# Decoder block on one core: projections, recurrence and attention in one stream over two token halves instead of three stages

## What is computed

```python
h = rmsnorm(x, norm_gain)
proj = h @ w_in                                    # 2048 x 6528
r, k, v, wd, ad, g = split(token_shift_lerp(p, mu))      # RWKV columns
decay = exp(-exp(w_log));  a = sigmoid(a0 + ad @ a_up);  kk = normalised k * k_k
# per head, per token:
sa = -S @ kk_t
S = S * w_t + outer(sa, b_t) + outer(v_t, k_t)
y = S @ r_t
y = groupnorm(y) * gain + bias + bonus;  y_rwkv = y * silu(g)
# attention: window 128, two kv heads, ALiBi slopes, a sink in the softmax
o = softmax([q k^T / 8 - slope * dist, sink]) @ v;  y_attn = o * silu(g)
out = rmsnorm(x + concat(y_rwkv, y_attn) @ w_out, final_gain)
```

## Time and profile before

| | |
|---|---|
| runs shown, median (lowest to highest) | 2253.88 us (2248.12 to 2255.84) |
| profiled execution: span, first to last instruction | 2249.4 us |
| outside the span, by the median | 4.5 us |
| PE, DVE, ACT, POOL busy in the span | 91%, 43%, 28%, 15% |
| DMA | 234 MB, mean 104 GB/s |

### The profile page before, as it was taken

One profiled execution on the slowest core, in us unless ns is written; L12 is line 12 of the kernel. 1 busy time (PEld: TensorE's weight loads), 2 busy tenths in 40 slices (PEclk: granted clock), 3 DMA queues, 4 the chain that ended last, 5 costly groups with the idle time before them and its releaser, 6 DMA issues. The chain is left out here.

```text
span 2249.4 us, 32629 instructions
## 1 busy us (share of the span) xinstructions
PE 2049.3 (91%) x12099; PEld 1715.2 (76%) x12099; DVE 965.8 (43%) x1225; ACT 620.1 (28%) x1295; POOL 327.2 (15%) x453
## 2 busy tenths in 40 slices
PE   6999999999999999999995788898889849998995
PEld 5788888888888888888884688787788737786874
DVE  5434243432434334343442565566566543334223
ACT  5321212112121121211210254344444443332331
POOL 1200000000000000000002113321332100114112
PEclk9999999999999999999998799999999979999997
DMA  8322222221333212322124344323332243444333
GB/s 289 126 63 80 84 85 87 76 88 59 84 94 84 85 56 75 94 84 85 56 84 135 84 130 125 98 90 122 124 97 104 60 142 125 140 140 168 120 119 120
DMA packets 135549, 234.03 MB, mean 104 GB/s; under 512 B 59936, under 2 KB 80416, under 8 KB 132896
## 3 DMA queue, kind: packets, MB, share of 16 engines
q1 hardware_dynamic: 120816, 180.85, 25.1%
q0 software_dynamic: 12336, 43.52, 7.2%
q10 hardware_dynamic: 2304, 8.39, 1.0%
HBM read 174.00 MB, written 58.72 MB: 103 GB/s over the span
## 5 line engine op out<-in xcount | busy, mean ns | idle before, releaser
L614 PE MATMUL psum_a<-a_x_hi,a_w_hi 128*128 128x512 f32 x1632 | 511.2, 394 | 20.4 <-DVE a_x_lo L433 17.0
L614 PE MATMUL psum_a<-a_x_lo,a_w_hi 128*128 128x512 f32 x1632 | 504.5, 390 | 0.0
L614 PE MATMUL psum_a<-a_x_hi,a_w_lo 128*128 128x512 f32 x1632 | 504.0, 390 | 0.0
L388 DVE TENSOR_TENSOR a_w_lo<-a_w_raw,a_w_hi 128x1024 fp32r<-128x1024 f32 x102 | 126.3, 1238 | 640.5 <-ACT a_w_hi L301 637.8
L614 PEld LDWEIGHTS psum_a<-a_x_hi,a_w_hi 128*128 128x128 f32 x1632 | 305.2, 189 | 96.7 <-issue 22.4
L614 PEld LDWEIGHTS psum_a<-a_x_lo,a_w_hi 128*128 128x128 f32 x1632 | 307.5, 188 | 64.6
L614 PEld LDWEIGHTS psum_a<-a_x_hi,a_w_lo 128*128 128x128 f32 x1632 | 307.4, 188 | 64.4
L301 ACT ACTIVATE a_w_hi<-a_w_raw 128x1024 fp32r<-128x1024 f32 x102 | 108.0, 1058 | 798.3 <-PE psum_a L614 789.2
L1957 PE MATMUL psum_c<-c_m_hi,c_w_hi 128*128 128x512 f32 x512 | 205.0, 400 | 31.9 <-DVE c_m_lo L1819 16.1
L1957 PE MATMUL psum_c<-c_m_lo,c_w_hi 128*128 128x512 f32 x512 | 201.8, 394 | 0.0
L1957 PE MATMUL psum_c<-c_m_hi,c_w_lo 128*128 128x512 f32 x512 | 201.5, 393 | 0.0
(11 more groups left out here) (202 smaller groups left out, 2443.6 us busy)
## 6 DMA issues: line engine op xcount, KB each, us to landing
a_w_raw<-in_w_in SPq DMA_DIRECT2D x102, 512.0 KB, 3.3
c_w_raw<-in_w_out SPq DMA_DIRECT2D x64, 512.0 KB, 4.9
b_qr_s<-scratch_QR SPq DMA_DIRECT2D x8, 1024.0 KB, 5.3
c_x_in<-in_x_t SPq DMA_DIRECT2D x32, 256.0 KB, 2.6
b_kb<-scratch_KB SPq DMA_DIRECT2D x6, 1024.0 KB, 4.7
b_qr<-scratch_QR SPq DMA_DIRECT2D x6, 1024.0 KB, 6.9
a_r<-in_x_t SPq DMA_DIRECT2D x8, 512.0 KB, 5.2
a_k<-in_x_t SPq DMA_DIRECT2D x8, 512.0 KB, 5.4
```

Source lines behind the costliest of these rows:

```text
L388: nc.vector.tensor_tensor(w_lo[half][:], w_raw[:], w_hi[half][:].bitcast(F32), ALU.subtract).then_inc(w_ready[half], 1)
L614: mm = nc.tensor.matmul(psum[:, 2 * parity + h], wt[half][:, cols], xt[:, c, h * HALF:(h + 1) * HALF], start=(c == 0 and wt is w_hi and xt ...
```

## The change

The three stages become one block with all instructions written out. Tokens are handled in two halves of 512. Each half's projection is 51 tiles of 48 products; then come 2 x 16 output tiles. A tile is loaded, split and used in quarters of 4 chunks (512 weight columns, 12 products); there are 536 quarters, and every engine walks the same list of them. SP loads a quarter three ahead of DVE's splitting, ACT and DVE split four quarters ahead of PE (`SPLIT` = 5 buffers). The weights of the input projection are loaded and split twice, once for each half.

A head pair's six tiles are an interval of 24 quarters. In interval j the engines make the channels of pair j and run recurrence and attention of pair j - 1 on chip: 512 tokens, 2 heads, 8 chunks. `at` is the quarter within an interval, 0 to 23; the steps `at` = 24 to 32 of the interval before fall on quarters 0 to 8 of the next one, and are worked on first. PE does a step's products before the quarter's 12 projection products, or after the first 6 of them (`between`); DVE and ACT do a step after splitting the weights of quarter + 4. The PE steps are: products at 0 and 1, turns 3, scores 5 and 9, z 6, turned probabilities 9 and 13, values 11 and 15, the five levels of the inverse 12, 14, 15, 16, 17, u 18, transition matrices 19, the eight steps of the chain 20 to 24, y 24, turning y 29; for the channels LoRA 1, norms 11 and 13, bonus 22.

The recurrence takes another form. The inverse is made in 64x64 blocks per head and chunk (`by_chunk`, the two chunks of a block of 128 tokens on opposite quadrants of partitions). From it come a transition matrix per chunk (`mt`) and a fresh part; so the state passes through the eight chunks by one 128x128 product and one DVE operation each (`chain`), and the outputs of all chunks are made together afterwards. The softmax is now divided before the probabilities are turned. Q, K, V, gates and the rest are no longer stored to DRAM; the 16x16 blocks and `MIX` still are. x is read again for each half; at three places (`FIRST`) the 16 chunks of x or of `MIX` are replaced in the same buffers, three staging buffers at a time. The mean squares of the first half are 16 products of 512 columns within tile 0.

```diff
-def stage_a(nc, io, scr, pc_all, consts):
...
-def stage_b(nc, io, scr, pc_all, cst, used=()):
...
-def stage_c(nc, io, scr, cst):
...
+PRE = 3
+PER = 6
+SPAN = 4 * PER
+INTERVALS = 2 * PAIRS
+H1 = PRE + PER * PAIRS
+OUT0 = 2 * H1
+OUT1 = OUT0 + KC
+SEQS = OUT1 + KC
+QUARTERS = 4 * SEQS
+FIRST = (0, H1, OUT0, OUT1)
+RAW, SPLIT, STAGE = 3, 5, 3
+TAIL = 33
...
+def base(i):
+    return 4 * PRE + SPAN * i + (4 * PRE if i >= PAIRS else 0)
...
+def program(nc, io, scr):
...
+        def current(gq):
+
+            return [(j, gq - base(j)) for j in range(INTERVALS + 1) if 0 <= gq - base(j) < TAIL]
...
+                def load_w(gq):
+                    if gq >= RAW:
+                        sp.wait_ge(w_ready, gq - RAW + 1)
+                    s, part_ = divmod(gq, 4)
+                    src = io["w_in"][s % H1, part_] if s < OUT0 else io["w_out"][(s - OUT0) % KC, part_]
+                    sp.dma_start(w_raw[gq % RAW][:], src).then_inc(w_landed[gq % RAW], 16)
...
+                def recurrence(i, at):
+                    if at == 2:
+                        sp.wait_ge(a_read, 2 * i + 2)
+                        for f in range(P // SUB):
...
+                    if at == 3:
+                        sp.wait_ge(l_out, 8 * 16 * (i + 1))
+                        sp.wait_ge(lev_full, 5 * i)
+                        sp.dma_start(sub_l, scr["L"].rearrange("f m s t -> (f m) s t")).then_inc(l_in, 16)
+                    if at == 8:
+                        sp.wait_ge(sub_done, i + 1)
...
+                    if at == 9:
+                        sp.wait_ge(x_out, 16 * (i + 1))
+                        sp.wait_ge(pool_inited, 1)
+                        for f in range(P // SUB):
...
+                def inverses(i):
+                    pool.wait_ge(l_in, 16 * (i + 1))
+                    pool.wait_ge(x_out, 16 * i)
+                    pool.wait_ge(u_full, 2 * i)
+                    then(nc.gpsimd.tensor_copy(sub_x[:, 0], sub_ident[:]))
+                    for s in range(SUB - 1):
...
+                        then(nc.gpsimd.tensor_tensor(t, left, right, ALU.mult))
+                        rows = sub_x[:, 0, s + 1:, 0:width]
+                        then(nc.gpsimd.tensor_tensor(rows, rows, t, ALU.subtract))
+                    then(nc.gpsimd.tensor_copy(sub_x[:, 1], sub_x[:, 0].rearrange("p s t -> p t s")))
+                    pool.sem_inc(sub_done, 1)
...
+                def high(gq):
+                    act.wait_ge(w_landed[gq % RAW], 16 * (gq // RAW + 1))
+                    if gq >= SPLIT:
+                        act.wait_ge(w_used, gq - SPLIT + 1)
+                    copy(w_hi[gq % SPLIT][:], w_raw[gq % RAW][:]).then_inc(w_high, 1)
...
+                def channels(j, at):
+                    n = j % PAIRS
+                    if at == 1:
+                        act.wait_ge(lora_done, 2 * j + 1)
+                        act.wait_ge(bonus_done, j)
+                        act.wait_ge(par_landed, 16)
+                        nc.scalar.activation(s1, psum[:, 2], ACT.Sigmoid, bias=p(n, "w0")).then_inc(sigma_w, 1)
+                        act.wait_ge(lora_done, 2 * j + 2)
+                        act.wait_ge(rkr_ready, j)
+                        nc.scalar.activation(a, psum[:, 3], ACT.Sigmoid, bias=p(n, "a0")).then_inc(sigma_a, 1)
+                    if at == 3:
+                        act.wait_ge(summed, j + 1)
...
+                        nc.scalar.activation(grow, sw, ACT.Exp, scale=DECAY).then_inc(exps, 1)
+                    if at == 5:
+                        act.wait_ge(k_ready, j + 1)
+                        nc.scalar.activation(s1, k, ACT.Square, scale=p(n, "k_k")).then_inc(squares, 1)
...
+                def exponentials(i, rnd):
+                    act.wait_ge(negmax, 2 * i + rnd + 1)
+                    for x in range(4):
+                        nc.scalar.activation(score[:, x], score[:, x], ACT.Exp, bias=top[:, 1, x:x + 1],
+                                             accum_out=top[:, 2, x:x + 1])
+                    nc.scalar.activation(top[:, 3], part[:], ACT.Exp).then_inc(p_ready, 1)
+
+                def turned_p(i, rnd):
+                    act.wait_ge(pt_full, 2 * i + rnd + 1)
+                    act.wait_ge(o_full, 2 * i + rnd)
+                    copy(pt[:, 0], psum[:, 4])
+                    copy(pt[:, 1], psum[:, 5]).then_inc(pt_read, 1)
+
+                def recurrence(i, at):
+                    if at == 3:
+                        act.wait_ge(t_full, 4 * i + 1)
+                        for m in range(2):
+                            act.wait_ge(t_full, 4 * i + m + 1)
+                            copy(late[:, 4 + m], psum[:, 6 + m]).then_inc(t_read, 1)
...
+                        act.wait_ge(t_full, 4 * i + 4)
+                        copy(kkt[:].rearrange("p m d -> p (m d)"), psum[:, 5]).then_inc(t_read, 1)
+                    if at == 6:
+                        for c in range(2):
...
+                def low(gq):
+                    dve.wait_ge(w_high, gq + 1)
+                    nc.vector.tensor_tensor(w_lo[gq % SPLIT][:], w_raw[gq % RAW][:], w_hi[gq % SPLIT][:].bitcast(F32),
+                                            ALU.subtract).then_inc(w_ready, 1)
...
+                def softmax_top(i, rnd):
+                    n = i % PAIRS
+                    then(nc.vector.tensor_reduce(top[:, 0], score[:], AX, ALU.max))
...
+                def softmax_norm(i, rnd):
+                    dve.wait_ge(p_ready, 2 * i + rnd + 1)
+                    then(nc.vector.tensor_tensor(part[:], top[:, 2], top[:, 3], ALU.add))
+                    then(nc.vector.reciprocal(part[:], part[:]))
+                    for x in range(4):
+                        ins = nc.vector.tensor_scalar(score[:, x], score[:, x], part[:, x:x + 1], None, ALU.mult)
+                    then(ins)
+                    dve.sem_inc(p_norm, 1)
...
+                def level(i, lev):
+                    dve.wait_ge(lev_full, 5 * i + lev + 1)
+                    for c in range(2):
+                        us = us_rows(c)
+                        bank = (6, 6, 6, 4, 6)[lev] + c
+                        src = psum[us, bank].rearrange("p (m t) -> p m t", t=C)
+                        if lev in (0, 3):
+                            mask = const("m16" if lev == 0 else "m32")[us]
...
+                def chain(i, m):
+                    n = i % PAIRS
+                    dve.wait_ge(state_full, NCH * i + m + 1)
+                    dst = states[:, m + 1] if m < NCH - 1 else state[:, n]
+                    then(nc.vector.scalar_tensor_tensor(dst, psum[:, 7, 0:HD], pc[:, i % 2, m:m + 1], fresh[:, m],
+                                                        ALU.mult, ALU.add))
+                    dve.sem_inc(state_new, 1)
...
+                    if at == 0:
+                        masked(i, 0)
+                    if at == 1:
+                        masked(i, 1)
+                    if at == 5:
+                        softmax_scores(i, 0)
+                    if at == 6:
+                        softmax_top(i, 0)
+                    if at == 8:
+                        softmax_norm(i, 0)
+                    if at == 9:
+                        softmax_scores(i, 1)
+                    if at == 10:
+                        softmax_top(i, 1)
+                    if at == 11:
+                        attended(i, 0)
+                    if at == 12:
+                        softmax_norm(i, 1)
+                        level(i, 0)
+                    if at == 14:
+                        level(i, 1)
+                    if at == 15:
+                        level(i, 2)
...
+                for gq in range(QUARTERS):
+                    if gq + 4 < QUARTERS:
+                        low(gq + 4)
+                    cg = chunk_group(gq)
+                    if cg:
+                        slices(*cg)
+                    for j, at in current(gq):
+                        if j >= 1:
+                            recurrence(j - 1, at, False)
+                        if j < INTERVALS:
+                            channels(j, at)
+                        if j >= 1:
+                            recurrence(j - 1, at, True)
+                    prepare(gq)
+                    u = gq // 4 - OUT0 - 1
+                    if u >= 0 and gq % 4 == 0:
+                        add(u)
...
+                def quarter(gq, between):
+                    s, part_ = divmod(gq, 4)
+                    if part_ == 0 and s >= 2:
+                        pe.wait_ge(tile_read, s - 1)
+                    pe.wait_ge(w_ready, gq + 1)
...
+                        if kk == 2:
+                            between()
+                        cols = slice(kk * P, (kk + 1) * P)
+                        for wt, xx in ((w_hi, x_hi), (w_hi, x_lo), (w_lo, x_hi)):
+                            mm = nc.tensor.matmul(psum[:, s % 2], wt[gq % SPLIT][:, cols], xx[:, c],
+                                                  start=(c == 0 and wt is w_hi and xx is x_hi),
```

(94 more changed lines are left out.)

2493 lines of the change are left out of this document (896 added, 1597 removed).

## The result

The changed kernel takes 2271.24 us (median of 4 runs, 2268.66 to 2272.44), the one before 2254.07 beside it: ratio 1.008, 95% interval 1.0066 to 1.0095. It is 0.8% slower; 2280 was forecast, 1.2% slower. The profiled execution has a span of 2266.9 us.

What follows compares the result with a forecast made beforehand. PE was taken as the bound, full in stages A and C but waiting in B. Projections 1458, full intervals 692, ends, start, means and exchanges gave span 2274, plus 4.5: 2280 us, 1.2% slower; range 2130 to 2410.

Steps and rivals of the forecast that it cites:

- The 4.5 us: Added to the forecast span of 2274 us, since the kernel before had span 2249.4 for a median of 2253.88.
- Small products on PE: Recurrence, attention and channel products among an interval's projections: 35.7 us, nothing hidden, quadrant products priced 0.0675 each from L1524.
- The stall at step 9: PE's turning of the first probabilities waits for DVE's division of the scores: 6.0 us per interval (0 to 9).
- 2 us of clock: After each stall of 6 us PE comes back at 1.2 GHz instead of 2.4: 2 us (0 to 4).
- Rival 1: The stall at step 9 isn't there: 120 us less, 2160 us (2100 to 2230), chance 0.28.
- Step 13: The spread norm comes late from DVE, behind division and level 0 of the inverse: 1.4 us per interval.
- step 21: The state chain on PE waits for the r tile: 1.0 us per interval.
- Rival 2: Quadrant pairs on PE run fully side by side, 0.057 us a product, all else as forecast: 2257 us, chance 0.07.
- Rival 3: Quadrant pairs don't run side by side, each product costs as L1511, 0.114: 2395 us (2330 to 2450), chance 0.20.
- What hides: Under PE: doubled weight loads cost nothing, POOL's inverses 12.4 us between steps 4 and 8, DVE some 76 us per interval.
- Exchanges: Three replacements of the x buffers, about 1.5 us a chunk, 16 chunks 6 us late, chain waiting at the second: 25 us.
- Start: PE's start 11 us, sixteen mean products in tile 0 15, DVE's work in the first tiles 5 (0 to 10).

Runs made afterwards that it cites:

- experiment 5: Changed kernel with by_chunk's 64x64 quadrant products issued all of one chunk, then all of the other, instead of alternately: 2340.76 us, 1.0387 of the kernel before.
- experiment 2: Changed kernel with the first turning of probabilities and the second scores moved from step 9 to 10 on all engines: 2211.67 us, 0.9813 of the kernel before.
- experiment 3: Changed kernel with first turning and second scores at step 11 instead of 9, values 12, second division 13, second turning 14: 2154.08 us, 0.9548 of the kernel before.
- experiment 7: Changed kernel with the moves of experiment 3, and weights split three quarters ahead instead of four from quarter 16 on: 2130.84 us, 0.9453 of the kernel before.
- experiments 7 and 9: experiment 7, and the same kernel with four staging buffers for x instead of three, which measured 2096.85 us, 0.9308 of the kernel before.
- experiment 10: experiment 7 with POOL sending the 16x16 inverses to DRAM and SP returning them before its next weight load: 2109.6 us, 0.9361 of the kernel before.
- experiment 8: Changed kernel with four staging buffers for the chunks of x instead of three, POOL making the unit blocks anew: 2237.26 us, 0.9929 of the kernel before.

## Why the prediction was right, step by step

PE's first projection records at the borders of the parts (tiles 3, 9, 102 and 108), and its last:

```profile
76.77 1.42 PE L1060 MATMUL psum<-x_hi,w_hi 128*128 128x512 f32 x1
...
149.30 0.39 PE L1060 MATMUL psum<-x_hi,w_hi 128*128 128x512 f32 x1
...
1841.07 0.50 PE L1060 MATMUL psum<-x_hi,w_hi 128*128 128x512 f32 x1
...
1944.86 0.50 PE L1060 MATMUL psum<-x_hi,w_hi 128*128 128x512 f32 x1
...
2239.21 0.39 PE L1060 MATMUL psum<-x_hi,w_lo 128*128 128x512 f32 x1
```

With 10.88 us a tile taken off, this is the sum beside the forecast's:

| beyond the projections' 1458 us | forecast | measured |
|---|---|---|
| start, mean products, first tiles (to 76.77, less 3 tiles) | 31 | 44 |
| interval 0 (7) and last recurrence alone (39) | 38 | 46 |
| 15 full intervals, without the exchanges (1841.07 - 149.30, less 93 tiles, less 35) | 692 | 645 |
| three exchanges of x (19, 16 and about 11, means included) | 27 | 46 |
| tail | 28 | 28 |

The 35 us of the first two exchanges are what those stretches take beyond the steady 108.2: half an interval 72.9 instead of 54.1, a whole one 124.1. Measured sum 809, forecast 816. That the total is so much better than its terms is luck: 47 us too much in the intervals stand against 40 too little at start, end and exchanges. The 4.5 us put on top of the span for the device time were too much as well: the profiled execution took 2268.66 us with a span of 2266.9, so 1.8. The 4.5 had set a median against the span of one execution.

- **Small products on PE, 35.7 us an interval.** Right in kind, 3.7 too much. With waits and lost clock taken off (6.0, 1.6, 1.2, 2.1) the interval of 108.2 leaves 97.3, so 32.0 beside the projections. Of the difference 1.7 is step 19 (0.038 instead of 0.09 a product), 0.5 the 16 products of y (0.039 instead of 0.0675), 0.8 the other 128 quadrant products at 0.061; the rest, some 0.7, is spread over the other terms. The choice that decided, L1524 and not L1511 as the nearest row, is shown by experiment 5: the order of issue makes the one price or the other.
- **The stall at step 9, 6.0 us, and 2 us of clock.** Right: 5.8 to 6.3 in the steady intervals; shown as a cause by experiments 2 and 3, the clock by the 2.1 us counted after the stalls and the 0.97 that became 1.00. The size to the tenth owes something to two counts that were too long by 2.7 us each. Rival 1, its absence, was wrong here; what it would give, 15 x 8 = 120 us, is what experiment 3 gave (117).
- **Step 13, 1.4; step 21, 1.0.** 1.6 and 1.2. The reason given for step 13, division and level 0 ahead of the norm, isn't refuted by the 1.3 us that stayed in experiment 3, since PE came 1.0 us earlier there; three quarters of lead instead of four took the wait away too. The chain's 1.2 us in every interval also meet, by a little, one of the forecast's own signs of being wrong (over 1 us in all), and at the exchanges of x it waits up to 4.7 us; PE isn't over 9 tenths from first to last slice either, but at 8 or 9.
- **Rival 2, full overlap of a quadrant pair, 0.057.** The rows say 0.061 where sets follow each other and 0.067 with the change to projections; the first is nearer to the rule of the Trainium skill's "TensorEngine Tiling (Array Packing)", Key Properties, than the forecast was. What the quadrant products were put too dear by is counted above. **Rival 3** (0.114) is wrong for this order and right for the other.
- **What hides.** Weights fetched and split twice cost PE nothing outside the exchanges. POOL's inverses were hidden, with the condition the prediction set, "unless PE runs faster than below": in experiments 7 and 9 it did, and 31 us of waits came; experiment 10 took them away by SP's and POOL's order of sending alone. DVE's 76 us an interval were 69 (411.40 in six).
- **Exchanges, 25 us (10 to 40).** The step that was off most in proportion, 46 us with the means instead of 27 and over its own upper bound of 40: a steady 1.5 us a chunk was assumed, a stop in every group of four is what happens (experiment 8), and the chain, put at one exchange, stood still in two, up to 4.7 us a time.
- **Start.** Some 13 us short. The first record is early, at 7.65 instead of 10.65. But tile 0 takes 20.8 us more than a plain one, 3.6 of them a wait for the constants, where 15 stood for its mean products; and in tiles 1 and 2 PE waited 5.7 us at 56.33 and 5.3 at 75.69 for DVE's reading of tiles and sums, where 5 were allowed in all.

## What to carry to other kernels

Where one engine is the bound and others feed it step by step, find for each step of its list when its input is ready and when it comes to it; a step asked two quarters early cost 117 us here, and moving it was a change of a few numbers. Take waits away together: each of these edits uncovered the next wait (step 13, then the return of the inverses), and a wait moved by reordering one queue may only go one link on. A prefetch depth must match the size of the group that is handled at once: three buffers for groups of four leave one bare transfer in each.

## What the runs showed of the hardware

- 64x64 products (L1198) whose neighbours in the queue use two opposite quadrants in turn cost 0.061 us each where another set follows, the same products grouped by quadrant 0.114 (experiment 5).
- Two sets that run through all four quadrants (both row halves, both column halves) cost less than either: the 32 of step 19 0.038 each, the 16 of y 0.039. In step 19 two neighbours share their stationary operand, in y none do, so that isn't what makes them cheap. That the four quadrants are the reason fits both, but no run changed it by itself.
- All 13 gaps of 5.8 us and more in the changed kernel's turnings bring the clock back at 1.2 GHz (1.97 us for eight turnings), and so does its one gap of 4.0. After the 13 gaps of 3.1 to 3.5 us in experiment 2 the same eight take 1.09 nine times, and in four of these the fall comes a group later. The length of the gap doesn't decide alone: in experiment 7 a gap of 2.1 us at 792.82 was followed by 1.97 us for a level that takes 1.15 after gaps of 2.0 to 2.6 elsewhere in that run.
